# Seven products for the gate projection, one unrolled feed-forward with one ring of weight pieces, and the sums of weight blocks on VectorE

## The chip, the cores and the metric

The kernel runs on one core of one Trainium2 chip. The metric is the device time of one execution in microseconds (us), lower is better. Every kernel is timed in several runs, and one more execution is profiled. TensorE (PE) multiplies, VectorE (DVE) and ScalarE (ACT) do the elementwise work, GpSimd (POOL) helps, and SyncE (SP) issues the loads.

## The reference

One inference step of a two-layer decoder trunk. The 512 prompt tokens and 8 x 8 sample tokens go through the same weights, 576 columns in all. Everything is fp32.

```python
def swiglu(x, w_in, w_out):
    gate, up = jnp.split(x @ w_in, 2, axis=-1)
    return (jax.nn.silu(gate) * up) @ w_out
...
def hybrid_layer(x, p, attn_fn, lru_h0, lru_buf, sc_buf):
    x = x + 0.5 * swiglu(rms_norm(x, p['ffn1_norm']), p['ffn1_w_in'], p['ffn1_w_out'])
    h = rms_norm(x, p['mix_norm'])
    q, k, v, f, bx_in, by_in, sb, sc, sx, g = split_columns(h @ p['w_in'])
...
    merged = (gates[:, :, 0] * (o_a @ wb[:WIDTH_A]) + gates[:, :, 1] * (o_b @ wb[WIDTH_A:WIDTH_A + WIDTH_B])
              + gates[:, :, 2] * (o_c @ wb[WIDTH_A + WIDTH_B:]))
    x = x + merged @ p['w_out']
    x = x + 0.5 * swiglu(rms_norm(x, p['ffn2_norm']), p['ffn2_w_in'], p['ffn2_w_out'])
    return x, (k, v, logf, h_last, lru_buf_new, sc_buf_new)
```

`D_MODEL` is 1024, `FFN_HIDDEN` 2816, and there are two layers, so four feed-forwards (`ffn1` and `ffn2` of each layer), each with 2 x 2816 input rows and 1024 output rows.

## The kernel before

**Three matmuls for one product.** An fp32 operand is split into a high part in the matmul's reduced format and the rest: ACT writes `hi = copy(w)`, DVE writes `lo = w - hi`. A product is three matmuls, hi x hi, hi x lo and lo x hi. One matmul has 128 x 128 weights and 288 columns, half of the 576. This holds for weights (`wraw` to `whi`, `wlo`) and activations (`hh`, `hl`; hidden values `ah`, `al`; sums of hidden values `bh`, `bl`).

**Order of the work.** Each engine runs its own in-order program, and semaphores join them. A *unit* is one load into one of the two halves of `wraw`, at most 1024 rows x 256 columns (1 MB). A *tile* is one PSUM result of 128 rows x 576 columns. Four PSUM slots turn over. SP loads unit n once unit n-2 has been split. `split_ahead` (ACT L873, DVE L1217) splits the weights of the tile after next.

**Feed-forward before.** Three parts, of 4, 4 and 3 steps. A step has two gate tiles and two up tiles (`plain`, L509; 48 matmuls each), on DVE the multiplication by the norm's factor (`tmp6`), on ACT Silu. After the four steps of part 0 and part 1 comes `seven`: the output product of 1024 hidden values as Strassen-like blocks, with seven block products in place of eight. One unit is `m = 0..6`, 4 chunks x 3 matmuls each (L549). It needs sums of weight blocks (`weight_sums` on GpSimd, L1749, 4 for each unit, 16 each part) and sums of hidden blocks, made by DVE at the end of each step (`moving_first`, `moving_second`, `moving_lo`, L1258). Its weights go through a ring of four pieces (`comb_split`, ACT L906, DVE L1249). ACT copies four of the products out of PSUM (L956 to L962), DVE adds them up (L1310 to L1323). Part 2 has 6 chunks and goes through `plain` and `update` (L1233, `hh` L889, `hl` L1238). GpSimd adds the squares for the next norm (L1736), and a norm ends with `root` on ACT (L877) and a reciprocal on DVE (L1223).

**Around it.** At the start DVE makes the first `hl`, then constants of the RG-LRU (`spt`, L1416 to L1424), then enters the layer loop. `past_forgets` on SP (L427) loads 16 small pages of old forget logits (`lfp`); DVE waits for them at L1448 and copies them at L1449, and goes on to the forget logits, for which PE waits at L669.

Of the kernel before, what the change touches and what calls it, by code (L numbers as in the profile page):

```python
# [21 lines left out]
F32 = mybir.dt.float32  # L22
# [79 lines left out]
DONE_NO = {0: 1, 1: 2, 2: 3, 4: 4, 5: 5}  # L102
# [4 lines left out]
PRE_TILES = 12  # L107


def make_plan():  # L110
# [34 lines left out]
def build(nc, t_in, t_out):  # L145
    S, plan = make_plan()
    with ExitStack() as ctx:
# [43 lines left out]
        with ExitStack() as m:  # L191
            ah = sb("ah", [P, 6, N], F32R, m)
            al = sb("al", [P, 6, N], F32R, m)
        with ExitStack() as m:

            bh = sb("bh", [P, 7, 4, HF], F32R, m)
            bl = sb("bl", [P, 7, 4, HF], F32R, m)
            kept = sb("kept", [P, 3, HF], F32, m)
            wsum = sb("wsum", [P, 4, 4 * P], F32, m)
        with ExitStack() as m:  # L200
# [4 lines left out]
            spt = [sb(f"spt{i}", [P, DEPTH, 4], F32, m) for i in range(5)]  # L205
        with ExitStack() as m:
            yout = sb("yout", [P, 5, D], F32, m)
        with ExitStack() as m:
            o = sb("o", [P, 12, N], F32, m)
            with ExitStack() as m2:  # L210
# [14 lines left out]
                cs = sb("cs", [P, PAST + ST], F32, m2)  # L225
                lf = sb("lf", [F_W, N], F32, m2)
# [6 lines left out]
                lfp = sb("lfp", [P, NPG, 2 * NS], F32, m2)  # L233
# [30 lines left out]
        wsum_ready, comb_hi, comb_lo = sem("wsum_ready"), sem("comb_hi"), sem("comb_lo")  # L264
        product_done, part_copied = sem("product_done"), sem("part_copied")
# [61 lines left out]
        def ring(buf, q):  # L327

            r = q % 4
            return buf[:, r // 2, r % 2 * 4 * P:(r % 2 + 1) * 4 * P].rearrange("p (k c) -> p k c", c=P)  # L330

        def block_of(u, kh, mh_):

            return wraw[:, u, :].rearrange("p (k h c) -> p h k c", h=2, c=256)[:, kh, :, mh_ * P:mh_ * P + P]

        def summed(j):
            return wsum[:, j, :].rearrange("p (k c) -> p k c", c=P)

        def weights_of(st, u, m):

            slot = (st.first_unit + u) % 2
            if m == 0:
                return block_of(slot, 0, 0)
            if m == 5:
                return block_of(slot, 1, 0)
            if m == 6:
                return block_of(slot, 1, 1)
# [1509 lines left out]
```

## Time and profile before

| | |
|---|---|
| median of 3 runs | 2886.69 us (2882.81 to 2886.81) |
| the profiled execution, its own time | 2886.48 us |
| its span, first to last instruction | 2884.8 us |
| busy share PE, PEld, DVE, ACT, POOL | 98%, 96%, 59%, 39%, 11% |
| chain that ended last | PE 93%, DVE 3%, issue 1%, ACT 1%, DVE's sequencer 1% |
| granted TensorE clock | 1.000 |

The time between the span and the execution's own time (1.7 us) lies around the program. A matmul's shown duration overlaps the next one's, so the pace is read from starts, or from a long stretch of the chain divided by its count. The same holds on DVE and ACT: an operation of 0.68 us is followed by the next 0.60 us after its start.

### The profile page before, as it was taken

The numbers are of one execution on the slowest core, as the hardware profiler recorded it, in microseconds if no ns is written. First come the engines' busy times: TensorE is split into PE (matmuls) and PEld (weight loads), VectorE is DVE, ScalarE is ACT, GpSimd is POOL, SyncE is SP. The second block draws the span as 40 slices with busy tenths as digits, with TensorE's granted clock in tenths as the row PEclk, the third lists the DMA queues.
The fourth block names the chain that finished last, engine by engine and source line by source line (L and its number), as shares of the span: only waits on it lengthen the run. The fifth ranks groups of instructions, "written<-read, shape, count | busy, mean of one in ns | idle before, by whom it ended". The sixth has DMA issues, their size and how long they took to land.

```text
span 2884.8 us, 56179 instructions
## 1 busy us (share of the span) xinstructions
PE 2829.6 (98%) x21280; PEld 2764.3 (96%) x21280; DVE 1693.6 (59%) x2441; ACT 1112.6 (39%) x1669; POOL 312.8 (11%) x232
## 2 busy tenths in 40 slices
PE   7999999999999999999999999999999999999999
PEld 6999999899999999999999999998889999999998
DVE  4564756676655446656556565576666445575654
ACT  4332423555522333333333333335554223333324
POOL 1121201000000111111102021100000001030301
PEclk9999999999999999999999999999999999999999
DMA  3222223333222222222222223233332222222222
GB/s 121 73 88 87 88 74 99 90 96 87 82 80 87 89 85 70 95 73 97 80 76 87 88 73 103 74 89 90 90 107 71 87 80 97 74 81 95 73 88 91
DMA packets 299060, 249.22 MB, mean 86 GB/s; under 512 B 20643, under 2 KB 296307, under 8 KB 298919
## 3 DMA queue, kind: packets, MB, share of 16 engines
q1 hardware_dynamic: 296775, 242.44, 27.2%
q0 software_dynamic: 2144, 4.98, 0.5%
q8 instruction: 79, 1.29, 0.2%
q14 instruction: 62, 0.51, 0.1%
HBM read 240.04 MB, written 7.34 MB: 86 GB/s over the span
## 4 chain that ended last, share of the span: by engine, by line
PE 93%; DVE 3%; issue 1%; ACT 1%; DVEq 1%; DMA 0%; POOLq 0%; ACTq 0%; SPq 0%
PE ps L509 74%; PE ps L549 11%; PE ps L709 1%; PE ps L648 1%; PE ps L647 1%; PE ps L649 1%; PE ps L774 1%; PE ps L727 1%; PE ps L689 1%; DVE bl L1258 1%; DVE tmp L1223 1%; DVE wlo L1249 1%; PE ps L696 0%; PE ps L711 0%; DMA xin<-in_x_sample 0%
## 5 line engine op out<-in xcount | busy, mean ns | idle before, releaser
L509 PE MATMUL ps<-hh,whi 128*128 128x288 f32 x4480 | 965.3, 297 | 11.5 <-DVE wlo L1217 5.0
L509 PE MATMUL ps<-hl,whi 128*128 128x288 f32 x4480 | 959.3, 296 | 0.0
L509 PE MATMUL ps<-hh,wlo 128*128 128x288 f32 x4480 | 959.2, 296 | 0.0
L873 ACT ACTIVATE whi<-wraw 128x1024 fp32r<-128x1024 f32 (+1 forms) x388 | 403.9, 1042 | 1162.5 <-PE ps L509 1136.0
L509 PEld LDWEIGHTS ps<-hh,whi 128*128 128x128 f32 x4480 | 722.0, 189 | 14.2 <-DVE wlo L1217 5.9
L509 PEld LDWEIGHTS ps<-hh,wlo 128*128 128x128 f32 x4480 | 722.1, 189 | 0.0
L509 PEld LDWEIGHTS ps<-hl,whi 128*128 128x128 f32 x4480 | 721.9, 189 | 0.0
L1217 DVE TENSOR_TENSOR wlo<-wraw,whi 128x1024 fp32r<-128x1024 f32 (+1 forms) x388 | 467.0, 1204 | 374.4 <-ACT whi L873 373.6
L1266 DVE TENSOR_TENSOR tmp<-tmp,ps 128x576 f32<-128x576 f32 x128 | 96.6, 754 | 344.9 <-PE ps L509 344.5
L549 PE MATMUL ps<-bh,whi 128*128 128x288 f32 x896 | 266.8, 298 | 18.3 <-ACT tmp L956 12.8
L549 PE MATMUL ps<-bl,whi 128*128 128x288 f32 x896 | 264.3, 295 | 0.0
L549 PE MATMUL ps<-bh,wlo 128*128 128x288 f32 x896 | 263.6, 294 | 0.0
L1749 POOL TENSOR_TENSOR wsum<-wraw 128x512 f32<-128x512 f32 x64 | 101.4, 1584 | 891.5 <-DMA wraw<-in_ffn_w_out 793.9
L549 PEld LDWEIGHTS ps<-bh,whi 128*128 128x128 f32 x896 | 167.9, 187 | 22.5 <-DVE bl L1258 14.7
L549 PEld LDWEIGHTS ps<-bh,wlo 128*128 128x128 f32 x896 | 168.7, 188 | 0.0
L549 PEld LDWEIGHTS ps<-bl,whi 128*128 128x128 f32 x896 | 168.2, 188 | 0.0
L1346 DVE TENSOR_TENSOR tmp<-tmp,ps 128x576 f32<-128x576 f32 x48 | 36.2, 755 | 149.6 <-PE ps L509 149.6
L1249 DVE TENSOR_TENSOR wlo<-wraw,whi 128x512 fp32r<-128x512 f32 x96 | 103.7, 1095 | 25.8 <-ACT whi L906 25.2
L1249 DVE TENSOR_TENSOR wlo<-wsum,whi 128x512 fp32r<-128x512 f32 x128 | 114.4, 899 | 5.0 <-ACT whi L906 4.7
L906 ACT ACTIVATE whi<-wsum 128x512 fp32r<-128x512 f32 x128 | 79.5, 627 | 69.4 <-PE ps L549 41.1
L1736 POOL TENSOR_TENSOR tmp<-tmp 128x576 f32<-128x576 f32 x49 | 82.7, 1689 | 156.8 <-ACT tmp L893 155.2
L1233 DVE SCALAR_TENSOR_TENSOR x<-ps,x 128x576 f32 x48 | 36.4, 758 | 102.5 <-PE ps L509 102.5
(333 smaller groups left out, 3549.9 us busy)
## 6 DMA issues: line engine op xcount, KB each, us to landing
wraw<-in_ffn_w_in SPq DMA_DIRECT2D x88, 1024.0 KB
wraw<-in_ffn_w_out SPq DMA_DIRECT2D x32, 1024.0 KB
wraw<-in_w_in SPq DMA_DIRECT2D x28, 1024.0 KB
wraw<-in_w_in SPq DMA_DIRECT2D x56, 512.0 KB
wraw<-in_ffn_w_out SPq DMA_DIRECT2D x16, 768.0 KB
wraw<-in_w_branch SPq DMA_DIRECT2D x24, 512.0 KB
wraw<-in_w_out SPq DMA_DIRECT2D x9, 1024.0 KB
kv<-in_cache_k SPq DMA_DIRECT2D x128, 64.0 KB, 1.8
```

What stands on the lines that cost most here:

```text
L509: last = pe.matmul(ps[slot][:, half, 0:HF], weights, rhs[:, k, half * HF:(half + 1) * HF], start=(start and c == 0 and n == 0), stop=(stop ...
L549: last = pe.matmul(bank, weights[:, kk, :], moving[:, x_, kk, :], start=(m in (0, 1, 5) and kk == 0 and t == 0), stop=(m in (3, 5, 6) and ...
L647: pe.matmul(out, hh[:, k, tok], rh, start=(k == 0), stop=False)
L873: act.activation(split_tile(into, j, rowwise), raw_tile(slot, j, rowwise), ACT.Copy).then_inc(hi_ready, 1)
L906: ins = act.activation(ring(whi, q), weights_of(st, u, m), ACT.Copy)
L1217: dve.tensor_tensor(split_tile(lo, j, rowwise), raw_tile(slot, j, rowwise), split_tile(hi, j, rowwise).bitcast(F32), ALU.subtract).then_in ...
L1233: dve.scalar_tensor_tensor(out=two(xm), in0=cols(st.slot(k)), scalar=half, in1=two(xm), op0=ALU.mult, op1=ALU.add)\
L1249: ins = dve.tensor_tensor(ring(wlo, q), weights_of(st, u, m), ring(whi, q).bitcast(F32), ALU.subtract)
L1266: dve.tensor_tensor(two(pf[:, 0:N]), two(tmp[6][:, 0:N]), cols(st.slot(k)), ALU.mult).then_inc(freed[st.slot(k)], 1)
L1346: dve.tensor_tensor(two(pf[:, 0:N]), two(tmp[6][:, 0:N]), cols(st_in.slot(k)), ALU.mult)\
L1736: pool.tensor_tensor(tmp[6][:, 0:N], tmp[6][:, 0:N], tmp[2 + m % 2][:, 0:N], ALU.add).then_inc(sq_added, 1)
L1749: pool.tensor_tensor(summed(j), x0, x1, op).then_inc(wsum_ready, 1)
```

## The change

The three parts of a feed-forward become one list of units, the same on all engines, with no inner loops. For each of 11 steps there is an `up` unit (plain, 2 tiles in 4 pieces) and a `gate` unit of seven products. After `up` 2, 5 and 8 come four `out` units of seven products each, over 4, 6 and 6 chunks of hidden values, and at the end four plain `last` units over 6 chunks. All weights go through the ring of four pieces. The gate's seven products need sums of the normed input's blocks (`th`, `tl`), which ACT and DVE make where `hh` and `hl` are made. All weight-block sums are DVE's, two pieces ahead of their split. `past_forgets` moves behind the loads of `fv`, and waits for the last tile of `ffn1`.

In the order of the engines SP, PE, ACT, DVE, GpSimd, behind the common lists:

```diff
+def ffn_units():
+    units = []
+    for s in range(STEPS):
+        units.append(("up", s, 0))
+        if s in (2, 5, 8):
+            units += [("out", s // 3, v) for v in range(4)]
+        units.append(("gate", s, 0))
+    return units + [("last", 3, v) for v in range(4)]
...
+        for m in range(7 if n in SEVEN_NO else 4):
+            items.append((n, m, at))
...
+for _j in range(4, len(ITEMS)):
+    _at = max(_at, max(i for i in range(_j) if ITEMS[i][2] % 4 == ITEMS[_j][2] % 4))
+    BEHIND[_at].append(_j)
...
             def past_forgets(L):
-                norm = S["ffn1norm"]
-                wait_apart(sp, filled[norm.slot(0)], norm.turn(0, L) + 1)
+                st, k = S["ffn1"], 2 * len(FFN_UNITS) - 1
+                wait_apart(sp, filled[st.slot(k)], st.turn(k, L) + 1)
...
                     if m in COPY_NO:
+                        pe.wait_ge(part_copied, copied(L, f, n, COPY_NO[m]))
...
+            def buffers_free(st, f, n, L):
+                kind, s, v = FFN_UNITS[n]
+                if kind == "out" and v == 0:
+                    act.wait_ge(mov_ready, blocks_ready(L, f, PART_STEPS[s][-1], 4))
+                elif kind == "gate" and FFN_UNITS[n - 1][0] == "out":
+                    act.wait_ge(freed[st.slot(2 * n - 2)], st.turn(2 * n - 2, L) + 1)
+                elif kind == "gate" and 0 < s <= 8:
+                    act.wait_ge(mov_ready, blocks_ready(L, f, s - 1, 4))
+                elif kind == "gate" and s > 8:
+                    act.wait_ge(a_ready, L * 12 + (6 * f + 2 * (s - 8)))
...
+                        if n in SEVEN_NO and m in (0, 1, 2, 4):
+                            parts(st, f, n, m, L)
+                        for j in BEHIND[i]:
+                            ring_split(st, f, j, L)
+                        if kind == "gate" and m == 5:
+                            act.activation(kept[:, 0:2, :], kept[:, 0:2, :], ACT.Silu).then_inc(silu_ready, 1)
+                        elif kind == "gate" and m == 6:
+                            if s < 8:
+                                moving_first(f, s, s - PART_STEPS[(s + 1) // 3][0], L)
+                            act.activation(tmp[5][:, 0:N], tmp[5][:, 0:N], ACT.Silu).then_inc(silu_ready, 1)
+                        elif kind == "up" and m == 0 and 0 < s <= 8:
+                            moving_second(f, s - 1, s - 1 - PART_STEPS[s // 3][0], L)
...
+            for kk in range(4):
+                norm_sums(0, kk)
...
+            def even_sums(c, g):
+                dve.tensor_tensor(tmp[4][:, 0:HF], x[:, c, HF:N], x[:, c, 0:HF], ALU.subtract)
+                dve.tensor_scalar(tmp[4][:, HF:N], x[:, c, HF:N], g, None, ALU.mult)
+            def odd_sums(c, ge, go):
+                dve.drain()
+                dve.tensor_scalar(tmp[0][:, 0:HF], tmp[4][:, 0:HF], ge, None, ALU.mult)
+                dve.scalar_tensor_tensor(out=tmp[1][:, 0:HF], ...)
+                dve.drain()
+                dve.scalar_tensor_tensor(out=tmp[0][:, HF:N], ...).then_inc(t_raw, 1)
+                dve.drain()
+                dve.scalar_tensor_tensor(out=tmp[1][:, HF:N], ...).then_inc(t_raw, 1)
+            def norm_sums_lo(at, kk):
+                for half in range(2):
+                    dve.wait_ge(t_hi, at + (2 * kk + half + 1))
+                    dve.tensor_tensor(tl[:, 2 * half:2 * half + 2, kk, :], ..., ALU.subtract).then_inc(t_ready, 1)
...
+            def weight_sum(st, f, i, L, first=None):
+                dve.drain()
+                dve.tensor_tensor(summed(n, m), x0, x1, op).then_inc(wsum_ready, 1)
...
+                        for j in BEHIND[i]:
+                            ring_split(st, f, j, L)
+                            if j + 2 < len(ITEMS):
+                                weight_sum(st, f, j + 2, L)
...
+                        elif kind == "last" and m % 2:
+                            if f == 0:
+                                norm_next(L, c, 8, L, 8)
+                            else:
+                                norm_next(L, c, 24, L + 1, 0)
+                                norm_sums(L, L * 16 + 16, c, L + 1, 0)
...
             first_weights(1)
+            for c in range(KD):
+                if c % 2 == 0:
+                    even_sums(c, gains[:, 0, c:c + 1])
+                else:
+                    odd_sums(c, gains[:, 0, c - 1:c], gains[:, 0, c:c + 1])
+                    norm_sums_lo(0, c // 2)
...
-            def weight_sums(st, g, L):
-                        pool.tensor_tensor(summed(j), x0, x1, op).then_inc(wsum_ready, 1)
-                        pool.drain()
```

`BEHIND[i]` lists the pieces that are split once PE has finished piece i: piece i + 4, and in front of `up` 3, 6 and 9, where a slot of the ring is skipped, the pieces come one or two at a time from the gate unit's products 4, 5 and 6. On DVE, `gate_part` adds the gate's products up and multiplies by the norm's factor (at m 3, 5 and 6), `even_hidden` at gate m 6 and `odd_hidden` at m 0 of the next `up` wait for Silu and make the hidden blocks, and `up_blocks` makes `moving_lo` 2, 3 and 4 at m 1, 2 and 3 of that `up`. `up_tile`, `out_part` and `added` do what the steps before did.

## Rows read from the trace of the kernel before

**Rows 1.** The page, busy share of each engine.
```profile
PE 2829.6 (98%) x21280; PEld 2764.3 (96%) x21280; DVE 1693.6 (59%) x2441; ACT 1112.6 (39%) x1669; POOL 312.8 (11%) x232
```

**Rows 2.** Chain in order of time, first feed-forward: start, us, what, count.
```profile
48.25 89.87 PE ps L509 x672
...
147.03 38.92 PE ps L549 x288
```

**Rows 3.** Timeline of DVE in an output unit: start, us, engine, line, operation.
```profile
172.94 0.68 DVE L1249 TENSOR_TENSOR wlo<-wsum,whi 128x512 fp32r<-128x512 f32 x1
173.54 0.44 DVE L1314 SCALAR_TENSOR_TENSOR x<-ps,x 128x288 f32<-128x288 f32 x1
173.91 0.44 DVE L1316 TENSOR_TENSOR x<-x,tmp 128x288 f32<-128x288 f32 x1
174.42 0.76 DVE L1318 TENSOR_TENSOR x<-x,tmp 128x576 f32<-128x576 f32 x1
175.10 0.45 DVE L1319 TENSOR_TENSOR x<-x,tmp 128x288 f32<-128x288 f32 x1
```

**Rows 4.** Timeline of ACT: a copy, a split, the next copy; a Silu.
```profile
142.26 0.39 ACT L956 ACTIVATE tmp<-ps 128x288 f32<-128x288 f32 x1
142.55 0.62 ACT L906 ACTIVATE whi<-wsum 128x512 fp32r<-128x512 f32 x1
143.07 0.40 ACT L958 ACTIVATE tmp<-ps 128x288 f32<-128x288 f32 x1
...
47.10 0.68 ACT L935 ACTIVATE tmp<-tmp 128x576 f32<-128x576 f32 x1 [4.49 <-DVE tmp L1266]
```

**Rows 5.** Timeline of DVE and of POOL where both work at once.
```profile
142.03 1.66 POOL L1749 TENSOR_TENSOR wsum<-wsum,wraw 128x512 f32<-128x512 f32 x1 [4.91 <-DVE wlo L1249]
...
142.47 1.77 DVE L1249 TENSOR_TENSOR wlo<-wsum,whi 128x512 fp32r<-128x512 f32 x1
```

**Rows 6.** Timelines at the end of layer 0: DVE, ACT, POOL; chain, last line.
```profile
1452.35 0.76 DVE L1233 SCALAR_TENSOR_TENSOR x<-ps,x 128x576 f32 x1 [1.80 <-PE ps L509]
...
1454.47 0.82 DVE L1238 SCALAR_TENSOR_TENSOR hl<-x,gains,hh  x1
1462.98 0.18 DVE L1428 COPY gain<-gains 128x26 f32 x1 [7.68 <-issue]
...
1454.88 1.69 POOL L1736 TENSOR_TENSOR tmp<-tmp 128x576 f32<-128x576 f32 x1 [3.05 <-ACT tmp L893]
...
1469.63 5.45 PE ps L509 x39
```

**Rows 7.** Timeline of DVE at the start of the kernel.
```profile
42.48 3.75 DVE L1223 RECIPROCAL tmp<-tmp 128x576 f32<-128x576 f32 x1
```

**Rows 8.** Timeline of ACT at the end of the kernel.
```profile
2873.16 1.06 ACT L873 ACTIVATE whi<-wraw 128x1024 fp32r<-128x1024 f32 x1 [2.21 <-PE ps L509]
...
2875.65 4.65 ACT L1204 ACTIVATE yout<-ps 128x1024 f32<-128x1024 f32 x5
```

**Rows 9.** Timelines of SP and DVE, and chain: the old forget logits.
```profile
378.75 17.84 SPq L427 DMA_DIRECT2D lfp<-in_cache_logf  x16
...
451.32 0.76 DVE L1233 SCALAR_TENSOR_TENSOR x<-ps,x 128x576 f32 x1 [1.80 <-PE ps L509]
...
464.43 0.16 DVE L1449 COPY lfp<-lfp 128x128 f32<-128x128 f32 x1
...
483.29 0.74 DVE L1465 SCALAR_TENSOR_TENSOR lf<-tmp 16x576 f32<-16x576 f32 x1
...
488.07 0.36 PE ps L669 x2
```

**Rows 10.** Timelines of SP and POOL: a load of 1 MB and its first user.
```profile
159.01 0.39 SPq L401 DMA_DIRECT2D wraw<-in_ffn_w_out  x1
...
164.13 1.36 POOL L1749 TENSOR_TENSOR wsum<-wraw 128x512 f32<-128x512 f32 x1 [2.26 <-DMA wraw<-in_ffn_w_out]
```

More of the change, by code:

```diff
@@ L204, in build @@
             cmask = sb("cmask", [P, 2 * P], F32, m)
-            spt = [sb(f"spt{i}", [P, DEPTH, 4], F32, m) for i in range(5)]
         with ExitStack() as m:
+            sb("over_th", [P, 8, 4 * HF], F32, m)
             yout = sb("yout", [P, 5, D], F32, m)
@@ L324, in split_tile, with ring @@
             return buf[:, j, 0:n * P].rearrange("p (k c) -> p k c", c=P)
[L327 to L341, printed above, removed]
+        def ring(buf, i):
+            r = ITEMS[i][2] % 4
+            half = chunks_of(ITEMS[i][0]) // 2
+            return buf[:, r // 2, r % 2 * 4 * P:(r % 2 * 4 + half) * P].rearrange("p (k c) -> p k c", c=P)
@@ L845, in _ @@
             post = DEPTH * plan["layer_tiles"] + PRE_TILES
-            last_st = S["ffn2"][-1][1]
-            for k in range(4):
-                pe.wait_ge(freed[last_st.slot(k)], last_st.turn(k, DEPTH - 1, 1) + 1)
+            last_st = S["ffn2"]
+            for k in range(2 * len(FFN_UNITS) - 4, 2 * len(FFN_UNITS)):
+                pe.wait_ge(freed[last_st.slot(k)], last_st.turn(k, DEPTH - 1) + 1)
             for b in range(5):
@@ new lines, in parts @@
+            def parts(st, f, n, m, L):
+                kind, s, v = FFN_UNITS[n]
+                first, second = ps[st.slot(2 * n)], ps[st.slot(2 * n + 1)]
+                if kind == "out":
+                    one, other = scratch(v)
+                    places, scale = (one[:, 0:HF], other[:, HF:N], one[:, HF:N], None, other[:, 0:HF]), 0.5
+                else:
+                    places, scale = (kept[:, 0, :], tmp[5][:, HF:N], kept[:, 1, :], None, tmp[2][:, 0:HF]), 1.0
+                if m == 0:
+                    buffers_free(st, f, n, L)
+                src = second[:, 0, 0:HF] if m == 1 else first[:, 0, 0:HF]
+                act.activation(places[m], src, ACT.Copy, scale=scale).then_inc(part_copied, 1)
@@ new lines, in added, with update @@
+            def added(st, k, L, i, c, half):
+                wait_tile(st, k, L, i)
+                dve.scalar_tensor_tensor(out=two(x[:, c, :]), in0=cols(st.slot(k)), scalar=half, in1=two(x[:, c, :]), op0=ALU.mult, op1=ALU.add)\
+                    .then_inc(freed[st.slot(k)], 1)
+            def update(st, L, h0, gain_row, gain_at):
+                for c in range(KD):
+                    i, k = divmod(c, 4)
+                    added(st, k, L, i, c, 1.0)
+                    split_ahead(st, k, L, i)
+                    norm_next(L, c, h0, gain_row, gain_at)
+                    norm_sums(L, L * 16 + 8, c, gain_row, gain_at)
@@ L1794, in _ @@
                 add_squares(L * 24 + 16)
-                for part in range(2):
-                    weight_sums(S["ffn2"][part][1], part_no(2, part), L)
                 add_squares(L * 24 + 24)
```

679 lines of the change are left out of this document (370 added, 309 removed).

## Prediction

> **What bounds the kernel now.** I read the page first. PE is busy for 98% of the span, DVE for 59%, GpSimd for 11% [rows 1]. So there is no slack on PE to win back, only work: the kernel gets faster when PE has fewer matmuls, as long as DVE and ACT can feed it. The chain gives PE's pace: 672 matmuls in 89.87 us, 0.1337 us each. It also shows a hole: that stretch ends at 138.1, the long run of 288 output matmuls begins at 147.0, and only 48 (6.4 us) lie between, so PE stood 2.5 us [rows 2]. All eight output stages of seven products begin like that. The timelines give the price of small operations, which decide this change.
>
> **Prices.** On DVE, from start to start: 512 columns 0.60, 288 columns 0.37, 576 columns 0.68, and 0.15 more where a drain lies between [rows 3]. That is a slope of 1.03 ns per column, so 256 columns cost 0.34 and 384 cost 0.47. On ACT: copy of 288 columns 0.29, split of 512 columns 0.52, and 0.59 for a Silu of 576 (0.68 shown, less the same overlap) [rows 4].
>
> **What PE loses.** Per feed-forward the gate had 11 x 96 = 1056 matmuls and gets 11 x 84 = 924; the output stays at 960 (672 + 288). 132 x 4 = 528 fewer, at 0.1337: **-70.6**. Each step is 12.8 (up) + 11.2 (gate) = 24.0 us on PE instead of 25.6. The eight holes go too, since an `up` unit stands between hidden values and their use: **-20.0**. What comes in their place is counted below.
>
> **A step of gate and up.** ACT's copy of a gate's product 0 waits until the step before has delivered `moving_lo` 4 (`buffers_free`), and PE's product 2 waits for that copy. Count DVE's queue from the end of product 5 of one gate to `moving_lo` 4 in `up` piece 3: nine operations of 288 columns (3.33), eight of 576 (5.44), six splits (3.60), four weight sums (2.40), ten drains (1.50), 16.3 together. It also stands twice behind ACT, which does `moving_first`, the second Silu and a split in that order (1.9), and later `moving_second` (0.4). That is 18.6, so it ends 17.05 after product 6, and with ACT's copy (0.39) PE may go on at 17.5. PE wants to at 12.8 + 3.2 = 16.0. So PE stands 1.5 in a step. This holds for steps 1, 3, 4, 6 and 7; in 3 and 6 the gate's product 6 has two splits behind it, 2.1. Per feed-forward 3 x 1.5 + 2 x 2.1 = 8.7: **+34.8**. Bounds: 0 (the queue ends 1.5 earlier) and 2 x 34.8.
>
> **Output units.** DVE has in each: five operations of 288 columns and one of 576 with two drains (2.8), seven splits, four sums with drains. Over 4 chunks (256-column pieces): 2.8 + 7 x 0.34 + 4 x 0.49 = 7.2 us, against PE's 42 x 0.1337 = 5.6. Over 6 chunks: 2.8 + 7 x 0.47 + 4 x 0.62 = 8.6 against 8.4. For part 0: three periods of 1.6 (4.8), 0.7 at the first copy, which waits for `moving_lo` 4, and 2.7 at the gate unit behind it, whose first copy waits for DVE to free the last output unit. That is 8.2, four times **+32.8**. Parts 1 and 2: 0.7 + 1.1 + 1.5 = 3.3, eight times **+26.4**. Bounds: 4.8 x 4 = 19 for both parts together (throughput alone), and 90 if each boundary costs two us more.
>
> **The start.** The eight chunks' sums stand in DVE's program in front of `spt` and of the reciprocal, which now starts right behind DVE's own queue, with no idle time shown [rows 7]. An even chunk costs 0.37 + 0.29; an odd one 1.94, a wait of 0.35 for ACT, and two times 0.68, 3.65. Four pairs are 17.2, and nothing covers them: PE has two tiles and then waits. **+17.3** with a small second stall.
>
> **The end of ffn2.** The same sums stand in the last units, tiles of 36 matmuls, 4.8 us. A tile's add starts, `hl` follows 2.12 later and takes 0.74 to the next; then GpSimd is adding the squares for 1.35 more [rows 6]. A DVE operation that meets GpSimd waits for it: 1.77 in place of 0.68, ending 0.55 after GpSimd's [rows 5]. So 2.86 + 1.35 + 0.66 + a split 0.47 = 5.34 for an even tile, 8.33 for an odd one, 13.7 for two where PE takes 9.6. Eight tiles end on DVE 58.5 after the stage's start, not some 3 after PE's 38.4. At the layer's boundary DVE then has its 7.68 without work and 0.9 of small operations [rows 6], the reciprocal 3.75, and 1.45 until the first gate piece is split: 72.4 against 55.8 now (PE goes on at 1469.63, 17.4 after the stage [rows 6]). **+17.2** with the second stall. At the kernel's end ACT's output copies start 2.5 after the last tile [rows 8], and come to stand behind `norm_sums`: 57.4 against 40.9, **+16.5**. Without GpSimd's share these are 6.4 and 5.7; that is their lower bound, 25 each the upper. The `out` stage has 6.4 us a tile, 12.8 for two, against 12.7 on DVE: no cost, by that margin; if it fails, 5 us each time. Of such meetings the Trainium skill (GPSIMD Engine Reference, Specifications) says that GpSimd's SBUF interfaces are shared with VectorE and contended by instructions with two SBUF inputs. By this rule, with which rows 5 agree, the sums would meet GpSimd and the operations on PSUM would not.
>
> **Old forget logits.** 16 loads take 17.84 to issue [rows 9], and now begin when the last tile of `ffn1` is filled (just before the add at 451.3), so DVE has them 19.5 later (estimate with 1.6 of landing), at 470.7 instead of 464.4. The forget logits were ready at 484.0 for a PE that came at 488.1 [rows 9]: 6.3 - 4.0 = 2.3, two layers, **+4.6** (0 to 9).
>
> **Hidden at no cost.** ACT has 4.6 + 1.2 of splits and copies and 1.2 of Silu in a step's gate. GpSimd's removed sums were off the chain. The loads: 1 MB is in use 5.1 after its issue [rows 10]; the gate's has 6.9 from the split that allows it to its first sum, and if it is late, all of DVE's queue is. The inner loops that go cost nothing that rows show. The Trainium skill (Runtime: NRT & Kernel Launch, Instruction fetch mechanics) says that a taken branch out of the fetched window costs a fetch, and that kernels prefer full unrolling. The 7.68 at the layer's loop agrees, but that loop stays.
>
> **Sum.** -70.6 - 20.0 + 34.8 + 32.8 + 26.4 + 17.3 + 17.2 + 16.5 + 4.6 = +59.0. The profiled execution took 2886.5 of its own time (its span and 1.7 around it), 0.2 below the median: 2945.5 for the one, **2946** for the other.
>
> **Rivals.**
> - *DVE's queue inside the feed-forward stays covered* (faster). If DVE and ACT deliver `moving_lo` 4 within 16.0 - 0.4 of product 6, and the output units' waits are swallowed by the ring's lead of three pieces, the terms 34.8, 32.8 and 26.4 go: 2946 - 94 = 2852. The point is 1.5 us in a queue of 18.6. For it: a ring that runs ahead, and the rates for whole steps (DVE some 20 of 24 us). Against it: 7.2 over 5.6 in part 0 is throughput, no latency. Chance 0.18.
> - *The step holds and GpSimd doesn't hinder DVE*, only the output units, the start and the loads cost: 2946 - 35 - 22 = 2889, about no change. For it: rows 5 show other operations than the sums. Chance 0.09.
> - *Loads come late.* Two `wraw` halves now turn over each 5.6 to 12.8 us, in DVE's in-order queue. If each of the 48 output units waits 1 us: 2994. Against it: 5.1 of 5.6 in the tightest case is for 1 MB, and these are 512 KB. Chance 0.10.
> - The forecast, slower by 15 to 105 us: 2905 to 2990, chance 0.63.
>
> The range reaches from inside the second rival to the third: 2870 to 2995. A measurement here can't tell under 0.2% (5.8 us) from no change. Faster: the first rival and a third of the second, 0.21. Same: 0.05. Slower: 0.74.
>
> **What would show it.** PE's groups in the gate's product loop should show idle time ended by ACT's copies (1.5 in twenty steps) and, in the output units over 4 chunks, by DVE's `wlo` splits. PE should wait about 20 us once near 45 to 65 us, and 30 at the layer's boundary. DVE's busy share should be above 80%, with `moving_lo` 4 the last before the copy. The small loads should end a DVE wait of 6 us. I am wrong if DVE reaches `moving_lo` 4 before `up` ends, if DVE's sums start in a free engine, or if an `out` unit over 4 chunks takes under 6 us.

## The result and the profile after

The changed kernel takes 3033.68 us (median of 4 runs, 3031.08 to 3035.2) against 2886.33 for the kernel before. The ratio is 1.0512, with a 95% interval of 1.0494 to 1.0531: **slower by 5.1%, 147.3 us**. The prediction said slower, by 59, in a range up to 2995. The direction is right and the size is wrong: 3033.68 lies outside the range and beyond every rival.

The page of the changed kernel: the span, the busy shares and the granted clock in 40 slices, the chain by engine, and two groups of matmuls with their idle time.

```profile
span 3032.3 us, 58941 instructions
...
PE 2832.7 (93%) x20752; PEld 2742.9 (90%) x20752; DVE 2153.0 (71%) x3685; ACT 1329.5 (44%) x2393; POOL 116.7 (4%) x104
...
PEclk8999999999999999999999999999999999999999
...
PE 55%; DVE 18%; DVEq 10%; issue 8%; ACT 6%; SPq 1%; ACTq 1%; DMA 0%; POOLq 0%
...
L656 PE MATMUL ps<-bh,whi 128*128 128x288 f32 x896 | 276.4, 309 | 42.3 <-DVE wlo L1409 24.9
...
L656 PE MATMUL ps<-th,whi 128*128 128x288 f32 x704 | 220.4, 313 | 70.1 <-ACT kept L1062 69.5
```

PE has 528 matmuls fewer than in [rows 1], as worked out, and yet its busy time is 3 us longer. So matmuls have become slower, not only rarer. PE was 93% of the chain, now 55%: DVE and its sequencer hold 28%. And DVE is at 71%, not at the 80% that the prediction named: it does not have to be full to stop PE. The gate's products lost 69.5 us in front of ACT's copies (L1062, `parts`).

**Where the time went**, from the starts of successive matmuls in the two traces. A gap over 0.29 us is idle time (less the 0.134 of the pace), one of 0.20 to 0.29 is a slow matmul. The slow ones are split by whether they start in a stretch at the lower granted clock.

| | before | after | difference | predicted |
|---|---|---|---|---|
| matmuls at 0.1337 | | | -70.4 | -70.6 |
| idle time of PE | 76.7 | 238.4 | +161.7 | +129.6 (149.6 - 20.0) |
| slow matmuls | 33.3 | 88.1 | +54.8 | nothing |
| of these, at the lower clock | 0 | 43.7 | +43.7 | nothing |
| of these, elsewhere | 33.3 | 44.4 | +11.1 | nothing |
| sum | | | +146.1 | +59.0 |

The spans differ by 147.5. **The larger part of the miss is the line of the slow matmuls, and half of the miss is the lower clock.** The 11.1 elsewhere are at the full clock. Most of these matmuls stand next to the first one of a product in the gate and output units and are held up by some 0.1 each. Without the weight sums (no_weight_sums, below) only some 2 to 3 of the 11 are left. The next rows are four stretches around the one hole at 209.4 in the changed kernel: bounds, length, busy time (and instructions) of PE, PE's loads, DVE, ACT and POOL, granted clock, DMA share, GB/s.

```profile
206.30:209.40 3.10, 3.10 (x26) 3.10 (x24) 3.01 (x6) 0.63 (x1) 0.00 (x0) 1.00 0.00 0
209.40:212.50 3.10, 1.15 (x6) 0.91 (x6) 2.10 (x5) 1.36 (x4) 0.00 (x0) 0.87 0.00 0
212.50:216.00 3.50, 3.50 (x19) 3.50 (x19) 1.14 (x3) 1.33 (x3) 0.00 (x0) 0.62 0.00 0
216.00:221.20 5.20, 5.20 (x41) 5.20 (x40) 3.63 (x7) 2.26 (x5) 0.00 (x0) 1.00 0.47 151
```

Behind the hole the granted clock falls from 1.00 to 0.5 (1.2 GHz in place of 2.4) for 3.4 us, from 211.7 to 215.1. In the 3.50 us of the third row PE starts 17 matmuls instead of 26 (x19 also counts two that were still under way). The changed kernel has 129.7 us at the lower level, in 29 stretches within its work, all but the first some 3.4 or 6.8 long and each behind one or more holes. The kernel before has none within its work, though it has 23 gaps of over 0.9 us. (The rows of the clock begin at 33 to 34 us; the first matmuls ahead of them are slow in both kernels.) The longest of these gaps behind 33 us is 2.92 idle, at 45.2; all others are under 2.0.

**The knot of a step**, just as the prediction drew it. Timelines of DVE, ACT and PE at the same hole: start, us, engine, line.

```profile
208.73 0.75 DVE L1419 TENSOR_TENSOR bl<-tmp,bh 128x576 fp32r<-128x576 f32 x1
209.39 0.75 DVE L1460 TENSOR_TENSOR tmp<-tmp,ps 128x576 f32<-128x576 f32 x1
210.06 0.68 DVE L1409 TENSOR_TENSOR wlo<-wsum,whi 128x512 fp32r<-128x512 f32 x1
210.66 0.45 DVE L1419 TENSOR_TENSOR bl<-tmp,bh 128x288 fp32r<-128x288 f32 x1
```

```profile
211.14 0.41 ACT L1062 ACTIVATE kept<-ps 128x288 f32<-128x288 f32 x1 [3.73 <-DVE bl L1419]
211.45 0.62 ACT L1021 ACTIVATE whi<-wsum 128x512 fp32r<-128x512 f32 x1
```

```profile
209.36 0.30 PE L656 MATMUL ps<-th,wlo 128*128 128x288 f32 x1
211.61 0.53 PE L656 MATMUL ps<-th,whi 128*128 128x288 f32 x1 [1.95 <-ACT kept L1062]
```

`moving_lo` 4 (210.66) is the last of DVE's queue, ACT's copy of product 0 has waited 3.73 for it, and PE's product 2 waits for the copy. The waits over the whole kernel: engine and line, releaser, us in total, times, longest.

```profile
ACT kept L1062 <- DVE bl L1419: 74.5, 20, 3.7
...
ACT kept L1062 <- PE ps L656: 54.0, 50, 2.0
PE ps L656 <- DVE wlo L1409: 50.6, 60, 18.6
ACT kept L1062 <- DVE x L1520: 39.6, 12, 3.3
...
ACT tmp L1062 <- DVE bl L1419: 29.1, 12, 3.1
...
DVE lfp L1652 <- DMA lfp<-in_cache_logf: 14.5, 2, 7.3
```

Twenty waits of ACT's copies in the gates are for `bl`: five steps in four feed-forwards, steps 1, 3, 4, 6 and 7. Twelve are for `x`: the three gate units that stand behind output units.

**Start and end.** The reciprocal of [rows 7] (42.48) and ACT's first output copy of [rows 8]:

```profile
59.06 3.75 DVE L1331 RECIPROCAL tmp<-tmp 128x576 f32<-128x576 f32 x1
```

```profile
3021.91 1.30 ACT L1001 ACTIVATE th<-tmp 128x576 fp32r<-128x576 f32 x2 [2.88 <-DVE tmp L1351]
3023.12 4.66 ACT L1312 ACTIVATE yout<-ps 128x1024 f32<-128x1024 f32 x5
```

PE goes on at 64.47 instead of 48.25.

### The profile page after: what moved, and what is told of

Its sections match the earlier page's. It is cut to its first block, busy times and chain, and to the rows that moved or that the text cites. A ratio compares the mean times of both kernels' runs of the same rounds, so it can differ in the third digit from the quotient of the medians.

```text
span 3032.3 us, 58941 instructions
## 1 busy us (share of the span) xinstructions
PE 2832.7 (93%) x20752; PEld 2742.9 (90%) x20752; DVE 2153.0 (71%) x3685; ACT 1329.5 (44%) x2393; POOL 116.7 (4%) x104
## 4 chain that ended last, share of the span: by engine, by line
PE 55%; DVE 18%; DVEq 10%; issue 8%; ACT 6%; SPq 1%; ACTq 1%; DMA 0%; POOLq 0%
PE ps L608 30%; PE ps L656 14%; PE ps L693 6%; DVE wlo L1409 6%; DVEq L1395 5%; ACT whi L1021 2%; DVE wsum L1400 2%; DVEq L1447 1%; DVE bl L1419 1%; DVEq L1514 1%; ACT tmp L1062 1%; DVE kept L1432 1%; PE ps L821 1%; ACT tmp L1082 1%; DVE tmp L1460 1%
## 5 line engine op out<-in xcount | busy, mean ns | idle before, releaser
L1409 DVE TENSOR_TENSOR wlo<-wraw,whi 128x512 fp32r<-128x512 f32 (+2 forms) x500 | 316.6, 635 | 216.1 <-ACT whi L1021 207.8
L1325 DVE TENSOR_TENSOR wlo<-wraw,whi 128x1024 fp32r<-128x1024 f32 (+1 forms) x188 | 221.2, 1177 | 318.2 <-ACT whi L985 317.4
L608 PE MATMUL ps<-hh,whi 128*128 128x288 f32 x1664 | 362.2, 299 | 0.0
L608 PE MATMUL ps<-hl,whi 128*128 128x288 f32 x1664 | 357.7, 297 | 0.0
L608 PE MATMUL ps<-hh,wlo 128*128 128x288 f32 x1664 | 357.7, 297 | 0.0
L1021 ACT ACTIVATE whi<-wraw 128x512 fp32r<-128x512 f32 (+2 forms) x500 | 283.6, 571 | 139.5 <-PE ps L656 89.4
L693 PE MATMUL ps<-hh,whi 128*128 128x288 f32 x1408 | 303.5, 297 | 8.9 <-DVE hl L1607 4.7
L693 PE MATMUL ps<-hl,whi 128*128 128x288 f32 x1408 | 302.9, 297 | 0.0
L693 PE MATMUL ps<-hh,wlo 128*128 128x288 f32 x1408 | 302.3, 296 | 0.0
L656 PE MATMUL ps<-th,whi 128*128 128x288 f32 x704 | 220.4, 313 | 70.1 <-ACT kept L1062 69.5
L608 PEld LDWEIGHTS ps<-hh,whi 128*128 128x128 f32 x1664 | 269.3, 190 | 0.9
L608 PEld LDWEIGHTS ps<-hh,wlo 128*128 128x128 f32 x1664 | 269.4, 190 | 0.0
L608 PEld LDWEIGHTS ps<-hl,whi 128*128 128x128 f32 x1664 | 269.4, 190 | 0.0
L693 PEld LDWEIGHTS ps<-hh,whi 128*128 128x128 f32 x1408 | 228.3, 190 | 9.8 <-DVE hl L1607 5.0
L693 PEld LDWEIGHTS ps<-hh,wlo 128*128 128x128 f32 x1408 | 228.3, 190 | 0.0
L693 PEld LDWEIGHTS ps<-hl,whi 128*128 128x128 f32 x1408 | 227.9, 190 | 0.0
```

Of the source, the lines that this page charges most:

```text
L608: last = pe.matmul(ps[slot][:, half, 0:HF], weights, rhs[:, k, half * HF:(half + 1) * HF], start=(start and c == 0 and n == 0), stop=(stop ...
L656: last = pe.matmul(bank, weights[:, kk, :], moving, start=(m in (0, 1, 5) and kk == 0 and t == 0), stop=(m in (3, 5, 6) and kk == half - 1 ...
L693: last = pe.matmul(ps[slot][:, e, 0:HF], weights[:, kk, :], moving[:, c, e * HF:(e + 1) * HF], start=(c == 0 and t == 0), stop=(c == 2 * h ...
L1021: ins = act.activation(ring(whi, i), weights_of(st, i), ACT.Copy)
L1325: dve.tensor_tensor(split_tile(lo, j, rowwise), raw_tile(slot, j, rowwise), split_tile(hi, j, rowwise).bitcast(F32), ALU.subtract).then_in ...
L1409: ins = dve.tensor_tensor(ring(wlo, i), weights_of(st, i), ring(whi, i).bitcast(F32), ALU.subtract)
```

## Experiments

Each ratio is to the kernel before, run beside it on the same chip.

**own_buffers.** ACT's copy of a product waits only for the buffer that it writes, and not, at product 0, for all of them.

```diff
-                if m == 0:
-                    buffers_free(st, f, n, L)
+                buffer_free(st, f, n, m, L)
...
+                elif m < 2 and s > 8:
+                    act.wait_ge(a_ready, L * 12 + (6 * f + 2 * (s - 8) - 1 + m))
+                elif m == 1 and FFN_UNITS[n - 1][0] == "out":
+                    act.wait_ge(freed[st.slot(2 * n - 2)], st.turn(2 * n - 2, L) + 1)
+                elif m < 2 and s > 0:
+                    act.wait_ge(mov_ready, blocks_ready(L, f, s - 1, (1, 3)[m]))
```

> The changed kernel (3033.7 us), but each copy of a product by ScalarE waits only for the last reader of the buffer that it writes itself, in place of one wait in front of product 0 for everything. My theory (one in-order queue of VectorE and ScalarE ends late at this wait, and each hole on TensorE is followed by a stretch at the lower clock): the idle time in the gate units of steps 1, 3, 4, 6 and 7 (48.9 us in sum) goes, some 15 us behind the output units go, and with them some 30 us of the slow pace: 2930 to 2950 us, granted clock above 0.99. Rival A (VectorE's throughput is what is short, so the wait only moves to the split behind it): above 3010 us. Rival B (the low clock does not come from the holes): the holes go, the low stretches stay, about 2970 us at a granted clock of 0.98.

2925.09 us, ratio 1.0136 (1.0119 to 1.0153): 108.6 less than the change, 5 below the range expected. Both rivals fall. The waits of ACT for `bl` are down from 29.1 + 74.5 to the one row

```profile
ACT tmp L1062 <- DVE bl L1419: 12.9, 12, 1.6
```

and with them go the holes in the gates. The idle time is 156.7, the slow matmuls 60.6, the time at the lower clock 61.4. So 82 of the 109 are idle time and 27 are slow matmuls. All of these are clock: the slow matmuls in low stretches fell from 43.7 to 15.0, those elsewhere stayed (44.4 and 45.6). Part by part, time over the pace (of it idle), in us for all four feed-forwards; a gate unit behind output units is counted with them:

| | after | own_buffers | no_weight_sums |
|---|---|---|---|
| gates 1, 3, 4, 6, 7 | 72.3 (48.9) | 3.7 (3.0) | 0 |
| output part 0, gate 2 | 52.9 (40.2) | 35.4 (28.4) | 15.1 (12.3) |
| output parts 1, 2, gates 5, 8 | 49.2 (39.9) | 24.7 (17.4) | 0 |
| up 0 with the norm | 33.0 (27.2) | 32.9 (25.7) | 29.7 (22.2) |
| last units | 26.0 (24.7) | 27.5 (24.6) | 27.5 (24.7) |

The work is the same, on the same engines, in the same order. Only the place of a wait is different.

**no_weight_sums.** The sums of weight blocks are left out; the products take single blocks in their place.

```diff
-            return summed(n, m)
+            return block_of(st, n, m % 2, m // 2 % 2)
...
-                elif n in SEVEN_NO and m < 5:
-                    act.wait_ge(wsum_ready, copied(L, f, n, m))
```

> The changed kernel without any sum of weight blocks (left out; the splits read a plain block instead, so the output is another). My theory: VectorE's queue gets 3.0 us shorter in a step and 2.0 to 2.5 us shorter in an output unit, so nearly all idle time in the feed-forwards but that at the start, at the ends and between the layers goes (some 129 us of 182), with most of the slow pace: 2855 to 2890 us. Rival (the unrolled code or the smaller loads hold TensorE up): above 2980 us, with the idle time where it was.

2870.61 us, ratio 0.9948 (0.9928 to 0.9968), 163 less, as expected. With 368 sums fewer the queue reaches `moving_lo` 4 in time even with the wait at product 0, and the table shows no time over the pace in the gates. That is what the prediction's rival of the covered queue supposed: a step's queue was too long by some 2 to 3 us, the output units' by some 1 to 2, and the 163 us hung on both. Even without these sums, and with 70 us of matmuls fewer, the kernel is only 0.5% faster than the one before.

**no_norm_sums.** The sums of the normed input's blocks are left out, so the gate reads single blocks.

```diff
-            if x_ in NORM_BLOCK:
-                return th[:, NORM_BLOCK[x_], kk, :], tl[:, NORM_BLOCK[x_], kk, :]
...
-                    norm_sums(L, L * 16 + 8, c, gain_row, gain_at)
...
-                                norm_sums(L, L * 16 + 16, c, L + 1, 0)
```

> The changed kernel without the sums of the normed input's blocks (left out; the gate's products read plain blocks of the input instead, so the output is another). My theory: the wait of 19 us at the start and the slow pace behind it (10), the late ends of ffn2 (10 at the kernel's end, 5 to 15 at the layer's boundary, most of the idle time in its last units) go, nothing else: 2965 to 2985 us. Rival (these sums were covered but for the start): 3005 to 3015 us.

2985.95 us, ratio 1.0348 (1.0327 to 1.0369): 47.7 less, 1 above the range expected. The terms of the start, the boundary and the end were 51.0 in the prediction, but that these agree is in part luck. In the trace some 40 us are gone at those places (24.3 of idle time in the `up` units, 11.9 in the last units, 2.4 between the layers, 1.2 behind the last matmul). Another 9 come from matmuls that start 1.2 ns closer together in the `up` and gate units, for which no run gives the reason. The expected 10 us of lower clock did not come: the slow matmuls in low stretches are 42.4 beside 43.7.

**sums_on_gpsimd.** All 368 sums back on GpSimd.

```diff
+            def weight_sums(st, f, L):
+                        pool.tensor_tensor(summed(n, m), x0, x1, op).then_inc(wsum_ready, 1)
+                        pool.drain()
```

> The changed kernel with all sums of weight blocks on GpSimd (368 of them, four for each unit of seven products), as far ahead as the three buffers allow. VectorE is freed of 0.75 us for each, but an operation of it that meets GpSimd waits for GpSimd (1.77 us in place of 0.68). My theory: the two cancel nearly, 2990 to 3060 us, with VectorE's 512-column splits 0.3 us or more longer on average. Rival (the sums' place is what costs): as without them, 2860 to 2910 us.

3038.02 us, ratio 1.0528 (1.0507 to 1.0549): the same as the change within the intervals, as expected. The part of the change that its name puts last is worth nothing by itself. Groups of this kernel's splits and sums, with the mean in ns:

```profile
L1408 DVE TENSOR_TENSOR wlo<-wsum,whi 128x512 fp32r<-128x512 f32 x176 | 156.4, 894 | 42.8 <-ACT whi L1021 42.4
L1957 POOL TENSOR_TENSOR wsum<-wraw 128x512 f32<-128x512 f32 x88 | 129.4, 1470 | 670.4 <-DVE wlo L1408 480.4 <-DMA wraw<-in_ffn_w_in 178.9 <-PE ps L693 8.1
```

and the same split in the changed kernel:

```profile
L1409 DVE TENSOR_TENSOR wlo<-wsum,whi 128x512 fp32r<-128x512 f32 x176 | 120.7, 688 | 40.9 <-ACT whi L1021 40.9
```

DVE no longer sums, but a split of 512 columns takes 0.89 in place of 0.69 on the mean where GpSimd sums, 0.2 more and not the 0.3 expected.

**holes_in_before.** The kernel before, with a wait in front of chunk 3 of a gate tile in three steps of each seven-product part: 24 holes and no other work.

```diff
+                                if c == 3:
+                                    pe.wait_ge(mov_ready, L * 64 + i * 4 + (16 * part_no(n, done // 8) - 2))
```

> The kernel before with extra waits and no extra work: in steps 1 to 3 of parts 0 and 1 of each feed-forward, PE waits in chunk 3 of the first gate tile until the step before has delivered moving_lo 2. That makes 24 holes in TensorE's stream of some 2 us each. Theory (each hole of 2 us and more is followed by some 3.4 us at the lower clock, which costs 1.6 more): 24 x (2.0 + 1.6) = 86 us longer than before, about 2972, with a granted clock below 1.00 behind most of the holes. Rival (a hole costs its own length alone, and the slow stretches of the changed kernel have another cause): 48 us, about 2934, and the granted clock stays 1.00.

2980.73 us, ratio 1.0326 (1.0305 to 1.0347): 95.1 longer. Idle time rose by 65.6 (2.7 a hole, where 2.0 was expected) and slow matmuls by 29.5, 27.2 of them in low stretches. There are 64.8 us at the lower clock, in 19 stretches: 17 behind the 24 holes, one behind a hole of 2.1 at the start and one behind a hole of 1.9 in an output unit. The kernel before has none. The rival (2934, clock at 1.00) falls. The stretches around the hole at 122.9 and the one at 94.5, columns as above:

```profile
118.00:122.90 4.90, 4.90 (x39) 4.90 (x38) 2.28 (x4) 1.06 (x1) 0.00 (x0) 1.00 0.00 0
122.90:126.80 3.90, 1.27 (x10) 1.03 (x9) 3.81 (x7) 1.59 (x3) 0.00 (x0) 1.00 0.10 8
126.80:130.20 3.40, 3.40 (x17) 3.40 (x16) 0.06 (x1) 0.00 (x0) 0.00 (x0) 0.50 0.88 299
130.20:135.00 4.80, 4.80 (x38) 4.80 (x38) 2.35 (x2) 1.64 (x2) 4.13 (x3) 1.00 0.00 0
...
94.50:97.50 3.00, 0.37 (x3) 0.13 (x3) 2.91 (x6) 1.59 (x3) 0.00 (x0) 1.00 0.00 0
97.50:101.00 3.50, 3.50 (x27) 3.50 (x28) 0.87 (x2) 0.00 (x0) 0.00 (x0) 1.00 0.79 271
```

So a hole by itself brings the lower clock, but not every one: behind the hole at 122.9 PE starts 14 matmuls in 3.40 us at 0.50, behind the equally long one at 94.5 it starts 26 in 3.50 at 1.00. The DMA share is high in both stretches (0.88 and 0.79), so it is not what tells them apart. The lower clock cost 27.2 us for 24 holes, 1.1 each, 41% on top of their own length. In the changed kernel it was 43.7 on 161.7, 27%. These are means: no_norm_sums has 34.5 us of idle time less than the change, most of it in one hole of 19, and nearly the same time lost at the lower clock.

**own_pool_part0** and **own_pool_all.** own_buffers with the sums of part 0's output units, or all sums, on GpSimd.

```diff
+def on_gpsimd(n):
+    kind, s, v = FFN_UNITS[n]
+    return kind == "out" and s == 0
...
-                if n not in SEVEN_NO or m not in SUM_AT:
+                if n not in SEVEN_NO or m not in SUM_AT or on_gpsimd(n):
```

> own_buffers with the weight sums of the four output units of part 0 alone back on GpSimd (64 of 368 sums). Theory (these units are bound by DVE's throughput, 7.2 us against PE's 5.6, and 4 sums with drains are 2.0 of it; a split that meets GpSimd takes up to 1.1 longer): DVE's work in such a unit falls to 5.2 plus one or two meetings of 0.6 to 1.1, about 6.3. So 1 us less in most of 16 units and a part of the low clock behind: 10 to 20 less, 2905 to 2915 us. Rival (meetings cost as much as the sums save, as with all 368 sums): 2922 to 2930.

> own_buffers with all 368 weight sums on GpSimd. Theory (with the knot at the copies gone, a step has some 3 us to spare on DVE, so sums there cost nothing and meetings neither; in output units of part 0 the sums save what the meetings cost): 2910 to 2930 us, within 15 of own_buffers, and gates without holes in both. Rival (DVE's splits at 0.8 to 0.9 us instead of 0.68 delay the ring in every unit): above 2935.

With part 0 alone 2919.31 us, ratio 1.0117 (1.01 to 1.0134); with all 2937.38, ratio 1.0176 (1.0155 to 1.0196). Part 0 gains 8.0 over its pace (35.4 to 27.4), short of the 10 to 20 forecast. The time is 5.8 less, between the theory's range and the rival's, and the intervals of the ratios overlap with own_buffers, so by the times no gain is shown. All sums on GpSimd lie 12 above own_buffers and above the range of the theory, as the rival said: in the gates it brings back 9.6 us over the pace, in up 0 5.4.

**own_lfp_ahead.** The 16 small loads two at a time behind the loads of up 3 to 10, into a buffer that is free then.

```diff
+                        if name == "ffn1" and 3 <= s < 3 + SB:
+                            past_forgets(L, s - 3)
...
-                past_forgets(L)
                 pr = S["pair"]
```

> own_buffers with the 16 small loads of old forget logits issued two at a time behind the loads of up 3 to 10 of ffn1, into a part of a buffer that is free then; DVE copies twice in place of once. Theory (between ffn1 and ffn2 the changed kernel lost 13.9 us, because DVE stood 7.3 in each layer for the last of these loads, PE 4.4, and PE ran slowly behind it): 14 less than own_buffers, about 2911 us, the DVE wait gone, and no hole of over 1 us between the feed-forwards. Rival A (the term of the prediction, 4.6, was right and the rest of the 13.9 is something else): 2920. Rival B (two more DMAs behind each load of SP make the weights late): at or above 2925.

2915.06 us beside 2881.68 for the kernel before, ratio 1.0113 (1.0096 to 1.013); from the ratios 7 us less than own_buffers, from the medians 10. The intervals of the ratios overlap; the trace is clearer. From PE's last matmul of `ffn1` to its first of `ffn2` own_buffers takes 591.15 and 591.43 us, this kernel 584.83 and 584.63: 13.1 less. DVE's wait is gone. Rows of own_buffers, then of this kernel:

```profile
486.53 0.23 DVE L1652 COPY lfp<-lfp 128x128 f32<-128x128 f32 x1 [7.15 <-DMA lfp<-in_cache_logf]
```

```profile
477.79 0.16 DVE L1655 COPY lfp<-fout 128x128 f32<-128x128 f32 x1
```

The feed-forwards of this execution are 4.1 us longer than own_buffers' in sum, where no work differs; the low stretches of the clock lie elsewhere. The same loads into a buffer of their own (own_lfp_early) gave no time: the buffer doesn't fit into SBUF beside the others.

**own_first_gate_plain.** own_buffers with step 0's gate as a plain product (48 matmuls more in all), the sums of the normed input between the pieces of up 0 and gate 0.

```diff
-SEVEN_NO = {... if u[0] in ("out", "gate"))}
+SEVEN_NO = {... if u[0] == "out" or u[0] == "gate" and u[1] > 0)}
...
+                        if i == 0:
+                            wait_done(dve, st, f, 0, L)
+                            norm_sums(L, f, 0)
+                        elif i in (1, 3, 5):
+                            norm_sums_lo(L * 16 + 8 * f, i // 2)
+                            norm_sums(L, f, i // 2 + 1)
```

> own_buffers with the gate of step 0 as a plain product (48 matmuls more in all four feed-forwards, 6.4 us), so that the sums of the normed input's blocks are needed only in step 1, and DVE makes them between the pieces of up 0 and gate 0, in place of the start of the kernel and of the last units. Theory (the sums cost 47.7 us because nothing covers them there, and a step without seven products has some 8 us of DVE's time to spare): 2925 - 47.7 + 6.4 = 2884 us, 2878 to 2896, about as the kernel before; PE idles some 3 us once in front of its first gate, not 19, and the kernel's end is as before. Rival (the 17 us of sums move the ring's splits back in steps 0 and 1, and PE waits there instead): 2905 or more, with holes in gate 0, up 1 and gate 1.

2922.34 us, ratio 1.0142 (1.0125 to 1.0159): no less than own_buffers. The theory fell, the rival holds. Up 0 lost 25.8 of its time over the pace, the last units 11.5, and what follows the last feed-forward shrank from 15.0 to 5.6. But gate 0 has 10.2 over its pace and the gates 1, 3, 4, 6 and 7 have 26.6 (own_buffers 4.9 and 3.7), nearly all of that in gate 1. Timelines of ACT, DVE and PE there:

```profile
73.36 0.69 ACT L1031 ACTIVATE bh<-kept 128x576 fp32r<-128x576 f32 x1 [4.35 <-DVE kept L1431]
73.96 0.67 ACT L1085 ACTIVATE tmp<-tmp 128x576 f32<-128x576 f32 x1
74.53 0.61 ACT L1023 ACTIVATE whi<-wraw 128x512 fp32r<-128x512 f32 x1
```

```profile
75.18 0.69 DVE L1405 TENSOR_TENSOR wlo<-wraw,whi 128x512 fp32r<-128x512 f32 x1 [1.85 <-ACT whi L1023]
```

```profile
81.32 0.60 PE L660 MATMUL ps<-th,whi 128*128 128x288 f32 x1 [3.55 <-DVE wlo L1405]
```

ACT stands 4.35 for DVE's hidden block with the ring's next split behind it, then DVE stands 1.85 for that split, and is busy without a break until just before the split for which PE waits. I read this as two engines that block each other in turn; no run takes the exchange away alone.

**three_mended.** The three mends (own_buffers, own_lfp_ahead, own_first_gate_plain) and own_pool_part0 together.

> The three at once, and the weight sums of the output units of part 0 on GpSimd (own_buffers, own_lfp_ahead, own_first_gate_plain, own_pool_part0). Theory (the costs stand apart in time and add up): 2884 - 14 - 6 = 2864 us, 0.7% faster than the kernel before, 2855 to 2875. Rival (the sums' saving is eaten in step 0, or one mend uncovers another wait): above 2880.

2898.96 us, ratio 1.0061 (1.0044 to 1.0078). It is, with sums_of_scaled_input (1.0062), the fastest version that leaves nothing out, and still slower than the kernel before. It lies 35 above the forecast, which took 2884 for the third mend where 2922 was measured. Against own_buffers it is some 22 faster by the ratios.

```profile
PE 2797.4 (97%) x20800; PEld 2709.2 (94%) x20800; DVE 2075.8 (72%) x3547; ACT 1319.1 (46%) x2357; POOL 174.4 (6%) x168
```

It has 134.1 us of idle time and 13.7 us at the lower clock. Its slow matmuls are 53.0, of which 5.2 are in low stretches.

**sums_of_scaled_input** and **sums_spread_out.** Two tries at the exchange in steps 0 and 1. The first scales the input on ACT, so that DVE's sums are four subtractions for each pair. The second also puts ACT's and DVE's steps one piece apart.

```diff
+                    ins = act.activation(h_part(2 * q, 2), x[:, 2 * kk + q, :], ACT.Copy, scale=norm_gain(L, 16 * f + 2 * kk + q))
+                ins.then_inc(h_scaled, 1)
...
+                dve.tensor_tensor(T1, e1, e0, ALU.subtract)
+                dve.tensor_tensor(T3, o1, e1, ALU.subtract)
```

```diff
-                            norm_sums_lo(L * 16 + 8 * f, i // 2)
-                            norm_sums(L, f, i // 2 + 1)
+                        elif i in (2, 4, 6, 8):
+                            norm_sums_lo(L * 16 + 8 * f, i // 2 - 1)
+                            if i < 8:
+                                norm_sums(L, f, i // 2)
```

> three_mended with cheaper sums of the normed input: ACT scales a pair of chunks once (two copies), so that DVE makes the four blocks of a pair with four subtractions of 288 columns and three drains in place of six operations and four drains. three_mended lost 11.0 us in gate 0 and 22.8 in gate 1 over the four feed-forwards, and DVE was busy there without a break. Theory (DVE's queue in step 0 is 26.5 us long against PE's 25.6, and it gets some 1 us shorter for each of four pairs): the holes in gates 0 and 1 go for the larger part, 20 to 28 us less, 2871 to 2879, faster than the kernel before by 0.1 to 0.4%. Rival (the hole in gate 1 hangs on ACT, which stands before moving_first with the next Silu and the ring's split behind it, and gets more to do here): 2890 or more.

> sums_of_scaled_input with each pair's steps one piece apart: ACT copies th behind its ring split one piece after DVE's sums, DVE makes tl one piece after that. In sums_of_scaled_input the two engines answered each other inside one piece: DVE stood 1.4 to 2.0 us for ACT's split, which stood behind ACT's copy of th, which waited 3.1 for DVE. Theory (without this exchange DVE's queue in step 0 is some 23.5 us against PE's 25.6, and both engines reach step 1 in time): the holes in gates 0 and 1 go for the larger part, 2870 to 2885 us, at or just below the kernel before. Rival (DVE's or ACT's work in these steps is too much in any order, since the ring's lead is three pieces): within 5 us of 2903.

2903.32 us, ratio 1.0062 (1.0045 to 1.0079), and 2908.02, ratio 1.0075 (1.0062 to 1.0089). Both theories fell, and both rivals hold: neither is faster than three_mended. In sums_spread_out gate 0 is at its pace (0.6 over), but the ups behind it have 15.4 over and gates 1, 3, 4, 6 and 7 have 31.5: the holes moved one unit on. Timelines of ACT and DVE:

```profile
61.91 1.26 ACT L1024 ACTIVATE th<-tmp 128x576 fp32r<-128x576 f32 x2 [3.10 <-DVE tmp L1380]
63.08 1.43 ACT L1017 ACTIVATE wsum<-x,gains 128x576 f32<-128x576 f32 x2
64.53 1.28 ACT L1104 ACT_TABLE_LOAD   x1
65.82 0.69 ACT L1104 ACTIVATE kept<-kept 128x576 f32<-128x576 f32 x1
66.41 1.14 ACT L1042 ACTIVATE whi<-wraw 128x512 fp32r<-128x512 f32 x2
```

```profile
67.06 0.69 DVE L1426 TENSOR_TENSOR wlo<-wraw,whi 128x512 fp32r<-128x512 f32 x1 [3.37 <-ACT whi L1042]
```

DVE stands 3.37 for a split that ACT makes late. ACT stood 3.10 for DVE, and then had 4.5 us of other work in front of that split: the copies of `th`, the scaling, a table load of 1.28 (one in each feed-forward, in front of its first Silu) and the Silu. Less work on DVE did not help here, and neither did putting the two engines' steps one piece apart.

## Why the prediction was right in direction and wrong in size

- **What PE loses (-70.6 and -20.0).** Right: -70.4 measured. The holes of the output stages are gone as such; they stand within the difference of idle time. The hole of 2.5 that the prediction read from [rows 2] is two, 1.75 at 141.0 and 0.86 at 146.0, which changes nothing in their sum.
- **A step of gate and up (+34.8): right mechanism, too small.** Steps and waits are the ones named, 20 times. In the step shown above PE was ready at 209.5, 16.0 after product 6 of the gate before (at 193.5, which is 96 matmuls of the up unit and 24 of the gate back at the pace), as worked out. `moving_lo` 4 ended 17.6 after it, forecast 17.05, and PE went on 18.1 after it, forecast 17.5. These 0.6 us in 18 make the hole 2.1 in place of 1.5. Over the twenty steps the idle time is 48.9. The bounds given (0 to 69.6) hold it.
- **Output units (+32.8 and +26.4): too small.** The unit over 4 chunks takes 7.7 on the mean (7.2 forecast), that over 6 chunks 9.5 (8.6). With the gate units behind them, idle time is 40.2 and 39.9, 21 more than the two terms. own_buffers shows the cause of a good part: ACT's copy at product 0 also waits at these boundaries for things that it does not need, and 34 of these 80 go with it. Without the sums of no_weight_sums 12.3 are left, all in part 0 and its gate: the rest was DVE's work in these units, as argued for part 0.
- **The step that failed: each hole was priced at its own length.** No term of the sum has PE's pace behind a hole. The row that the pace came from, 0.1337 [rows 2], is one without long holes, and behind the holes of 1.75 and 0.86 the 288 matmuls of [rows 2] took 38.92, 0.135 each: the trace of before gave no sign of it. The runs put it at 43.7 us, with 11.1 more of short hold-ups at the full clock that no term has either. That the lower clock comes from the holes and not from the ring, the sums or the new order, holes_in_before shows: 24 holes in the old kernel bring 64.8 us of it. It also explains why own_buffers gave back 109 where its idle time fell by 82. The second fault is in the terms of idle time, 32 too small in sum, as the lines around this one show.
- **The start (+17.3).** Right: PE goes on 16.2 later, and part of what follows is at the lower clock.
- **The layer's boundary (+17.2): too large.** From the start of the last units to PE's going on it was 55.8, forecast 72.4, measured 67.6 (1482.48 to 1550.09), +11.8. The prediction let DVE's whole 7.68 without work follow its queue; measured it is 2.47:

```profile
1541.79 0.18 DVE L1631 COPY gain<-gains 128x26 f32 x1 [2.47 <-issue]
```

- **The kernel's end (+16.5).** Right: 55.9 from the start of the last units (2967.26) to ACT's output copies, 57.4 forecast, so +15.0. With GpSimd's squares beside it an operation of 288 columns takes long here, as argued; with GpSimd done it takes 0.36:

```profile
3007.81 1.36 DVE L1348 TENSOR_SCALAR tmp<-tmp,gains 128x288 f32<-128x288 f32 x1
...
3016.46 0.36 DVE L1343 TENSOR_SCALAR tmp<-x,gains 128x288 f32<-128x288 f32 x1
```

- **Old forget logits (+4.6): too small.** 13.9 between the feed-forwards, of which own_lfp_ahead gives back 13.1. The term counted the DVE wait as 6.3 with 4.0 of it hidden. The wait is 7.3, and PE had a hole of 4.4 in each layer and a slow stretch behind it.
- **Hidden at no cost.** Right for the loads: no wait of the ring is for `wraw`. The rival of late loads (2994) was nearest in size, but for a cause that the trace excludes. The rival without GpSimd's hindrance (2889) falls: the operation of 288 columns above takes 1.36 and not 0.36 beside it. That hindrance and the work it saves cancel for the weight sums: on DVE or on GpSimd makes no difference in the change (3034 and 3038).

The terms for idle time were 129.6 against 161.7 measured, short by 32; the clock adds 44 and the short hold-ups 11; together 87, and 59 + 87 = 146. The mended version is not faster than the kernel before because its 64 us of matmuls less are eaten by 57 of idle time more (134.1 against 76.7) and 20 of slow matmuls more (53.0 against 33.3, only 5.2 of it at the lower clock). What stays open is whether that can be avoided. A version whose sums of the input are covered without an exchange between ACT and DVE wasn't found, and one with more pieces in the ring wasn't tried.

## What to carry to other kernels

A wait for several buffers should stand where each buffer is written, not once at the first of them: that alone was 109 of 147 us here. When PE is at 98%, a change that saves its work has to be priced by the queues that feed it, and in those some 2 us over the slack, in twenty steps, came back as twenty holes (48.9 us of idle time). And a hole is to be priced above its length: here 1.3 to 1.4 times on the mean, read from the slow matmuls at the lower granted clock behind it. Look in the trace for in-order engines that wait for each other in turn, whatever their busy shares say: here DVE at 71% and ACT at 44% held PE up. What such an exchange costs by itself was not measured.

## What the runs showed of the hardware that was not expected

- The granted clock fell to 0.5 behind holes in TensorE's stream and was mostly back at 1.00 some 3.4 us later. Of the 24 holes of 2.8 us in holes_in_before 17 were followed by such a stretch and 7, equally long, were not; the runs don't show what tells them apart.
- GpSimd's sums of 512 columns (1.47 us) stretched DVE's splits of SBUF operands from 0.69 to 0.89 on the mean, and DVE's sums of 0.69 cost about as much as that: the choice of the engine came out even in the changed kernel (3034 and 3038), and 12 us worse on GpSimd in own_buffers.
